# Two heads of an attention pair in turns: score blocks and weighted sums issued block by block instead of head by head

## What is computed

```python
# stick: stick-breaking attention
z = einsum('bhtd,bhsd->bhts', qb, kb) * scale
log_keep = where(causal, -softplus(z), 0.0)
log_w = log_sigmoid(z) + cumsum(log_keep, reverse=True) - log_keep
o = einsum('bhts,bhsd->bhtd', where(causal, exp(log_w), 0.0), vb)

# moba: with 256 tokens one block only, so causal softmax attention with a distance penalty
s_own = einsum('bhcd,bhkd->bhck', qc, k_own) * scale - slopes * dist_own
o = einsum('bhck,bhkd->bhcd', softmax(where(dist_own >= 0, s_own, NEG_INF)), v_own)

# fox: causal softmax attention with a forget gate, c the running sum of log f
sc = einsum('bhqd,bhkd->bhqk', qb, k) * scale + cq[..., None] - c[:, :, None, :]
o = einsum('bhqk,bhkd->bhqd', softmax(where(kpos <= tq, sc, NEG_INF)), v)
```

## Time and profile before

| | us |
|---|---|
| median of 3 runs | 1336.31 |
| lowest and highest of them | 1331.77 and 1337.28 |
| span of the profiled execution | 1335.6 |
| busy: TensorE multiplications (PE) | 1284.8 (96%) |
| busy: TensorE weight loads (PEld) | 1066.8 (80%) |
| busy: VectorE (DVE) | 749.2 (56%) |
| busy: ScalarE (ACT) | 654.5 (49%) |
| mean granted TensorE clock | 0.985 of full speed |

### The profile page before, as it was taken

How to read it: one execution, slowest core, us unless ns; L and a number is a source line. 1 busy time by engine, 2 the same in 40 slices (tenths; PEclk the granted TensorE clock), 3 DMA queues, 4 the chain that set the end, 5 groups by cost and what they waited for, 6 DMA issues and landing times.

```text
span 1335.6 us, 19780 instructions
## 1 busy us (share of the span) xinstructions
PE 1284.8 (96%) x6530; PEld 1066.8 (80%) x6534; DVE 749.2 (56%) x1146; ACT 654.5 (49%) x1092; POOL 48.6 (4%) x105
## 2 busy tenths in 40 slices
PE   6999999999999999999999999999999999999997
PEld 4788887997878778888778877888878787788885
DVE  4455555444686655555557765555562666655543
ACT  5444446566644444444574655544462344644442
POOL 1000000121120010000000000000000000000000
PEclk9999999999999999999999999999998899999999
DMA  6755554335565536655634456564622335564641
GB/s 212 269 188 188 189 172 154 101 108 180 185 207 169 180 119 197 190 189 184 190 124 119 134 189 217 161 209 155 216 82 62 87 97 164 176 217 156 211 153 60
DMA packets 174416, 219.05 MB, mean 164 GB/s; under 512 B 9644, under 2 KB 104472, under 8 KB 174120
## 3 DMA queue, kind: packets, MB, share of 16 engines
q1 hardware_dynamic: 173112, 213.20, 50.2%
q0 software_dynamic: 960, 4.28, 0.8%
q10 hardware_dynamic: 304, 1.05, 0.2%
HBM read 217.43 MB, written 1.05 MB: 164 GB/s over the span
## 4 chain that ended last, share of the span: by engine, by line
PE 84%; DVE 7%; ACT 4%; DMA 2%; issue 2%; ACTq 0%; SPq 0%; DVEq 0%; POOL 0%; POOLq 0%
PE bank L1166 75%; DVE w_lo L792 3%; PE bank L1233 2%; ACT w_hi L509 1%; PE bank L1188 1%; PE bank L1343 1%; DMA raw<-in_ff_w_up 1%; DVE xt_lo L822 1%; PE bank L1304 1%; PE bank L1330 1%; PE bank L1303 1%; ACT xt_hi L534 1%; PE bank L1310 1%; PE bank L1308 1%; ACT work L588 1%
## 5 line engine op out<-in xcount | busy, mean ns | idle before, releaser
L792 DVE TENSOR_TENSOR w_lo<-raw,w_hi 128x512 fp32r<-128x512 f32 (+1 forms) x496 | 496.6, 1036 | 183.6 <-ACT w_hi L509 178.2
L509 ACT ACTIVATE w_hi<-raw 128x512 fp32r<-128x512 f32 (+1 forms) x496 | 422.8, 899 | 102.3 <-DMA raw<-in_w_down 28.5
L1166 PE MATMUL bank<-w_hi,xt_lo 128*128 128x512 f32 x864 | 344.1, 398 | 11.0 <-DVE work L838 4.1
L1166 PE MATMUL bank<-w_lo,xt_hi 128*128 128x512 f32 x864 | 338.7, 392 | 0.0
L1166 PE MATMUL bank<-w_hi,xt_hi 128*128 128x512 f32 x864 | 338.6, 392 | 0.0
L1166 PEld LDWEIGHTS bank<-w_hi,xt_lo 128*128 128x128 f32 x864 | 163.4, 189 | 49.8 <-issue 11.2
L1166 PEld LDWEIGHTS bank<-w_lo,xt_hi 128*128 128x128 f32 x864 | 163.2, 189 | 34.9
L1166 PEld LDWEIGHTS bank<-w_hi,xt_hi 128*128 128x128 f32 x864 | 163.3, 189 | 32.2
L1166 PE MATMUL bank<-w_hi,ht_lo 128*128 128x512 f32 x432 | 168.8, 391 | 6.9 <-DVE ht_lo L848 6.9
L1166 PE MATMUL bank<-w_lo,ht_hi 128*128 128x512 f32 x432 | 168.3, 390 | 0.0
L1166 PE MATMUL bank<-w_hi,ht_hi 128*128 128x512 f32 x432 | 168.3, 390 | 0.0
(11 more groups left out here) (184 smaller groups left out, 1208.0 us busy)
## 6 DMA issues: line engine op xcount, KB each, us to landing
raw<-in_w_up SPq DMA_DIRECT2D x64, 512.0 KB, 4.4
raw<-in_w_down SPq DMA_DIRECT2D x64, 512.0 KB, 5.2
raw<-in_ff_w_gate SPq DMA_DIRECT2D x88, 256.0 KB, 3.6
raw<-in_ff_w_up SPq DMA_DIRECT2D x88, 256.0 KB, 4.2
raw<-in_ff_w_down SPq DMA_DIRECT2D x88, 256.0 KB, 3.4
raw<-in_w_in SPq DMA_DIRECT2D x40, 512.0 KB, 4.4
raw<-in_w_in SPq DMA_DIRECT2D x32, 256.0 KB, 3.0
raw<-in_moba_w_qkv SPq DMA_DIRECT2D x32, 256.0 KB, 3.1
```

Source lines behind the costliest of these rows:

```text
L509: act.activation(w_hi[:, c % RING, 0:w], raw[:, c % RAW, 0:w], ACT.Copy).then_inc(s["hi_ready"], 1)
L792: dve.tensor_tensor(w_lo[:, c % RING, 0:w], raw[:, c % RAW, 0:w], w_hi[:, c % RING, 0:w].bitcast(F32), ALU.subtract).then_inc(s["lo_ready" ...
L1166: ins = pe.matmul(dst, p, q, start=first and n == 0, stop=last and n == 2)
```

## The change

`scores` issues both heads' first blocks, then both second blocks; in fox the products with `c` of head 0 and then of head 1 stand behind all four. `weighted` waits once, for the weights of both heads, and then issues both first blocks and both second blocks. No operation is added or removed, and the signals still come with each head's last product.

```diff
                 def scores(pr, e):
                     pe.wait_ge(s["qt_done"], at(phase, "qt_done") + pr + 1)
                     pe.wait_ge(s["kt_done"], at(phase, "kt_done") + pr + 1)
+                    qk = []
                     for h in range(2):
                         rows = slice(h * DH, (h + 1) * DH)
-                        q, k, z = qt[rows, e, :], kt[rows, e, :], z_bank(e, h)
-                        if kind == "stick":
-
-                            pe.matmul(z[:, 0:S], k[:, 0:P], q[:, 0:S], start=True, stop=True)
-                            ins = pe.matmul(z[:, S:3 * P], k[:, P:S], q[:, P:S], start=False, stop=True,
-                                            skip_group_check=True)
...
+                        qk.append((qt[rows, e, :], kt[rows, e, :], z_bank(e, h)))
+                    if kind == "stick":
+
+                        for q, k, z in qk:
                             pe.matmul(z[:, 0:S], k[:, 0:P], q[:, 0:S], start=True, stop=True)
+                        for q, k, z in qk:
+                            pe.matmul(z[:, S:3 * P], k[:, P:S], q[:, P:S], start=False, stop=True,
+                                      skip_group_check=True).then_inc(s["z_ready"], 1)
+                        return
+
+                    for q, k, z in qk:
+                        pe.matmul(z[:, 0:P], q[:, 0:P], k[:, 0:P], start=True, stop=True)
+                    for h, (q, k, z) in enumerate(qk):
+                        ins = pe.matmul(z[:, P:3 * P], q[:, P:S], k[:, 0:S], start=False,
+                                        stop=True, skip_group_check=True)
+                        if kind == "moba":
+                            ins.then_inc(s["z_ready"], 1)
+                    if kind == "fox":
+                        for h, (q, k, z) in enumerate(qk):
+                            c = c_row[0:1, ds((2 * pr + h) * S, S)]
+                            pe.matmul(z[:, 0:P], nones[0:1, :], c_row[0:1, ds((2 * pr + h) * S, P)],
+                                      start=False, stop=True, skip_group_check=True)
+                            pe.matmul(z[:, P:3 * P], nones[0:1, :], c, start=False, stop=True,
+                                      skip_group_check=True).then_inc(s["z_ready"], 1)
...
                 def weighted(pr, e):
 
                     pe.wait_ge(s["v_done"], at(phase, "v_done") + pr + 1)
+                    if kind == "stick":
+                        pe.wait_ge(s["wm_done"], at(phase, "wm_done") + 2 * pr + 2)
+                    else:
+                        pe.wait_ge(s["w_done"], hp + 2 * pr + 2)
                     for h in range(2):
-                        if kind == "stick":
-                            pe.wait_ge(s["wm_done"], at(phase, "wm_done") + 2 * pr + h + 1)
-                        else:
-                            pe.wait_ge(s["w_done"], hp + 2 * pr + h + 1)
...
-                        ins = pe.matmul(y_bank[rows, P:S], vn[:, e, 1, cols], work[2][:, h, S:3 * P],
+                    for h in range(2):
+                        rows = slice(h * DH, (h + 1) * DH)
+                        ins = pe.matmul(y_bank[rows, P:S], vn[:, e, 1, rows], work[2][:, h, S:3 * P],
                                         start=False, stop=True)
                     ins.then_inc(s["y_ready"], 1)
```

More of the change, by code:

```diff
@@ L1312, in scores @@
-                        ins.then_inc(s["z_ready"], 1)
+                        for q, k, z in qk:
[9 more added lines that the diff above has]
+                            ins.then_inc(s["z_ready"], 1)
@@ L1336, in weighted @@
                     pe.wait_ge(s["v_done"], at(phase, "v_done") + pr + 1)
+                    if kind == "stick":
+                        pe.wait_ge(s["wm_done"], at(phase, "wm_done") + 2 * pr + 2)
+                    else:
+                        pe.wait_ge(s["w_done"], hp + 2 * pr + 2)
                     for h in range(2):
-                        if kind == "stick":
-                            pe.wait_ge(s["wm_done"], at(phase, "wm_done") + 2 * pr + h + 1)
-                        else:
-                            pe.wait_ge(s["w_done"], hp + 2 * pr + h + 1)
-                        rows, cols = slice(h * DH, (h + 1) * DH), slice(h * DH, (h + 1) * DH)
-                        pe.matmul(y_bank[rows, 0:S], vn[:, e, 0, cols], work[2][:, h, 0:S],
+                        rows = slice(h * DH, (h + 1) * DH)
+                        pe.matmul(y_bank[rows, 0:S], vn[:, e, 0, rows], work[2][:, h, 0:S],
                                   start=True, stop=False)
-                        ins = pe.matmul(y_bank[rows, P:S], vn[:, e, 1, cols], work[2][:, h, S:3 * P],
+                    for h in range(2):
+                        rows = slice(h * DH, (h + 1) * DH)
+                        ins = pe.matmul(y_bank[rows, P:S], vn[:, e, 1, rows], work[2][:, h, S:3 * P],
                                         start=False, stop=True)
```

## The result

| | before | changed |
|---|---|---|
| median, us | 1335.67 (4 runs) | 1323.73 (4 runs) |
| lowest and highest, us | 1331.77 and 1337.28 | 1322.58 and 1324.82 |
| span of the profiled execution, us | 1335.6 | 1322.3 |
| mean granted TensorE clock | 0.985 | 0.990 |

A forecast was written before the change was run, and what follows sets the result against it. TensorE, 96% of the 1335.6 us span, was taken as the bound. 6.0 + 1.87 + 0.95 - 0.04 = 8.8 us gives 1326.8; with the median 0.7 above the span, 1327.5 us, range 1323 to 1334 (8 in 10).

The forecast's parts named there:

- The order that runs already: Stick and moba scores (16 groups) and weighted sums in the loops: the chip already pairs the heads, so 0 us.
- Fox at full clock: Fox scores, six pairs: group falls from 3.37 to 2.37 us, saving 1.00 us each, 6.0 us (4.9 by the upper bound).
- The split behind it: New fox score group: 0.86 us for paired 64-row products plus 1.51 us for two serial one-row parts, 2.37 us.
- The half-clock group: Fox, second pair's scores, 6.30 us at half clock: saves in proportion, 1.87 us (1.5 by the upper bound).
- The first pair: Fox, first pair's scores before the softmax wait: head 1's signal comes earlier, saving 0.95 us (0.8 by the upper bound).
- Slack: Fox loop, VectorE's weights ready 0.88 us before the transposes: slack stays within 0.1 us, so no new wait.
- The clock: Fox loop at full clock: TensorE's two falls to half clock, 3.4 us long, stay in the sum unchanged.
- my rival: Fox loop: one-row products in one stretch bring a fall after all six cycles, four more costing 6.0 us: 1333.5; chance 15%.
- The new wait: Last weighted sums of each phase: head 0 waits for head 1's weights, costing 0.01 us, three times: 0.04 us.
- The rule against the trace: Scores: the skill's strict program order would mean gains in all phases, 1319.5; the trace shows pairing already, and was followed.

The follow-up runs named there:

- The second experiment: Changed kernel with fox's scores put back into the old order; stick and moba scores and all weighted sums alternate: 1337.02 us, ratio 1.0009 to the kernel before.
- the first experiment: Kernel before with only fox's one-row c products moved behind both heads' 64-row products, which stay head by head: 1324.19 us, ratio 0.9908.
- third experiment: Changed kernel, but fox's heads alternate with the c products in between, keeping all three inner borders: 1326.28 us, ratio 0.9926.
- the old order without borders: Kernel before, head by head, with zero-padded c tile, 64-row c products in each head's half, fox loop written out: 1322.49 us, ratio 0.9894.
- three and one: Changed kernel with 64-row c products in each head's half, ordered three products of head 0, three of head 1, then one each: 1319.81 us.
- the better kernel: Changed kernel with c in a zero-padded 128-partition tile, so c products use each head's own 64 rows; fox loop written out: 1316.71 us, ratio 0.9853.
- two and two: Changed kernel with 64-row c products in each head's half, ordered two score products per head, then two c products per head: 1317.54 us, ratio 0.9862.

## Why the prediction was right and wrong

**The order that runs already: right.** Stick and moba, 0 us, and the loops' weighted sums, 0 us. The second experiment puts them together at a ratio of 1.0009. Read closely, each of these groups did become 0.007 us shorter (0.860 to 0.853 and 0.808 to 0.801), since head 1 starts 0.007 instead of 0.013 us behind head 0: about 0.3 us in 40 groups.

**Fox at full clock: right.** New group 2.37 us forecast, 2.35 to 2.36 measured. Five cycle lengths lie at 9.94 or 9.95. The split behind it (0.86 + 1.51) shows line by line, and the first and third experiment confirm both terms.

**The half-clock group: 1.87 forecast, 2.07 measured** for its cycle, 17.23 to 15.16 us. The group itself went from 6.30 to 4.43 us, 1.87 less, as forecast. The other 0.2 us lie behind it, in the 36 multiplications that took 4.82 and now 4.61 us: fewer of them ran at half clock. **The first pair:** 0.95 forecast, 0.96 measured. **Slack: right.** No new wait ahead of the transposes.

**The clock: the step that failed.** My sum left the number of falls in the loop as it was, at two. It went to none, and that is 2 x 1.5 = 3.0 us that my sum put at nothing. With it 1327.5 becomes 1324.5 us, against 1323.73 measured. The rest is mostly the base: with a fourth run the median of the kernel before moved from 1336.31 to 1335.67. From the first transposes of the loop to the end of the last scores, before took 1113.17 - 1034.11 = 79.1 us and the changed kernel 1099.84 - 1031.93 = 67.9 us. Of these 11.2 us, 8.2 are the shorter groups (forecast: 7.9) and 3.0 the falls. Worse than the zero was the reason in my rival: one-row products in one piece would make falls likelier. In the changed kernel and in the first experiment they stand in one piece of 1.5 us, and neither had a fall in six cycles. In both kernels with the old group of fox two stretches at half clock followed its groups, and there the one-row products take 1.7 us while each head's 64-row products use half of the array's rows alone. With the heads in turns and the borders kept, the one-row products also take 1.7 us, 0.64 + 1.06, but the 64-row products run in pairs, and there was no fall. So the one-row products alone don't make the falls. Little use of the array fits all twelve profiles, but I counted only its one-row part and overlooked that the change fills the array during the 64-row part. This cause is supported, not shown: how it works no run tells.

The timed runs bear the falls out beyond the profiles. The mean granted clock of the kernel before is 0.983 to 0.989 in its 27 runs beside the experiments, and 0.984 to 0.988 in nine of the ten runs with only fox in the old order. The changed kernel's four have 0.990 to 0.992. This mean takes in every half-clock stretch of a run, not the loop's alone.

My reason for the half clock at the start of fox, that TensorE waits for the first softmax, doesn't hold by itself. In the kernel before the clock fell 2.6 us into that wait, in the changed kernel 0.4 us into it, and in the kernel with only fox in the old order at 1028.7 us, while TensorE still multiplied by line 1314:

```profile
1028.52 0.83 PE L1314 MATMUL bank<-c_row,nones 1*128 1x256 f32 x2
```

**The new wait: sized too low.** I priced the last weighted sums of a phase at 0.01 us each. From the scores to what follows the sums it is 307.48 to 309.99 before, and now, by the timeline of the changed kernel's stick:

```profile
306.88 0.70 PE L1300 MATMUL bank<-qt,kt 64*128 64x256 f32 x4
...
308.69 0.65 PE L1350 MATMUL bank<-work,vn 128*64 128x256 f32 x4 [0.89 <-POOL work L422]
...
309.49 0.50 PE L1166 MATMUL bank<-w_hi,xt_lo 128*128 128x512 f32 x1
```

2.61 against 2.51 us: 0.10 us. In moba and fox it is 0.12 and 0.10, so 0.3 in all. It eats what the 0.007 us per group give.

**The rule against the trace** (multiplications strictly in program order): following the trace was right, and the first experiment makes it plain. But the order is not free either: the reach of two products is a limit I did not know of, and my theory for the old order without borders failed on it.

**The spread.** The changed kernel's runs lie 2.2 us apart, the kernel before's 5.5. I would have taken the falls in the loop for the cause, but the kernel with only the one-row products moved, whose profile has none, spreads over 5.3 us as well; with four runs each the cause stays open.

**The spans.** They differ by 13.3 us, more than the medians. Ahead of the first scores of fox the changed kernel is 1.2 us early (1026.27 against 1027.49). There the kernel before has two stretches of half clock at other places (at 50 and 494 us) and the changed kernel one (at 776); these are not the change's. Then come the first pair's 1.0 and the loop's 11.2 us. From the last scores of fox to the end both take 222.4 us.

## What to carry to other kernels

Before alternating work between two halves of TensorE's array, look at the timeline of the kernel as it is: if the lines already come as x4, the alternation is done. What hinders it is a product with another number of rows in between (0.2 us at each border here, and the pairing lost), or a distance of more than two fp32 products to the other half's work. A small operand padded with zeros to the neighbours' rows can be cheaper than a product with one row: here it gave another 7 us.

## What the runs showed of the hardware that I had not expected

- The reach: with two, three and four fp32 products of head 0 in front, head 1's first started 0.01, 0.31 and 0.74 us behind head 0's.
- Two heads that share all 128 rows and differ in columns ran side by side too: four of line 1343, then four of 1345, in 0.80 us. The last two weight loads of line 1343 started at 252.73 and 252.74 us, while its first two multiplications, on the same rows, ran from 252.68 to 253.12. The Trainium skill (TensorE: Matmul & The Clock Gate, Part 3: Packing small matmuls — row/col tiling) has weight loads overlap with running multiplications only between different rows of the array, and multiplications in strict program order. This trace disagrees with both.
- TensorE, busy throughout, was held at 1.2 GHz for 3.4 us at a time behind groups of 3.37 us with 1.7 us of one-row products and unpaired 64-row products, and behind groups of 3.67 us with 2.8 us of one-row products. It was not in the loops of the other nine kernels, with 1.7 us of one-row products in 2.75, 1.5 in 2.4 or in 3.8, or less. How often it happens would take more executions than these to say, and what exactly is measured stays open.
- The half clock at the start of fox had different lengths too: 17.1 us with only fox in the old order and with the one row twice, 13.7 in the kernel before, in the changed one and in the two that keep all of its one-row products, 10.2 with one row in each half and with 64 rows in the old order, 6.8 with the 64-row products three times and with three and one, 3.4 in the better kernel and with two and two. Kernels with the same fox code differ by 3.4 us here (17.1 and 13.7), so single profiles don't rank neighbours.
- Another sort of stretch comes behind waits. Behind the loop four kernels have 3.4 us at half clock just behind waits: the better one (from 1104.6 us on), those with two and two and with three and one, and the one with only fox in the old order. In the better one these are waits of 0.7 us for ScalarE and 1.0 us for VectorE. The changed kernel has the same two waits and no fall there.
